# One Gram product for both lanes of a delta head, decays by ScalarE, and the next head's weight parts made inside the inversion

## The reference, cut to what matters

```
decay = exp(gc_i - gc_j) for i >= j           # gc: running sum of g in the chunk
lmat  = (beta_i * k_i . k_j) * decay, i > j   # strictly triangular
sol   = (I + lmat)^-1 [v * beta | k * beta * exp(gc)]        -> u, w
per chunk: v_new = u - w S;  o = (q exp(gc)) S + ((q k^T) * decay) v_new
           S = S * exp(gc_last) + (k * exp(gc_last - gc))^T v_new
```

## Time and profile before

| | |
|---|---|
| median of 3 runs | 4918.99 us (4915.6 to 4931.08) |
| the profiled execution's own time | 4920.18 us |
| its span | 4918.3 us |
| TensorE busy | 4060.4 us, 83% |
| VectorE busy | 3022.4 us, 61% |
| ScalarE busy | 1895.9 us, 39% |
| GpSimd busy | 768.2 us, 16% |
| mean granted TensorE clock | 0.894 of full speed |

### The profile page before, as it was taken

One profiled execution on the slowest core, in us unless ns is written; L12 is line 12 of the kernel. 1 busy time (PEld: TensorE's weight loads), 2 busy tenths in 40 slices (PEclk: granted clock), 3 DMA queues, 4 the chain that ended last, 5 costly groups with the idle time before them and its releaser, 6 DMA issues. The chain is left out here.

```text
span 4918.3 us, 52675 instructions
## 1 busy us (share of the span) xinstructions
PE 4060.4 (83%) x19068; PEld 3233.2 (66%) x19068; DVE 3022.4 (61%) x3602; ACT 1895.9 (39%) x2236; POOL 768.2 (16%) x364
## 2 busy tenths in 40 slices
PE   3956799958997999678888888849999597699995
PEld 2723587734734777467777877737888476588884
DVE  6753477344835874355555555538999543699995
ACT  2032332212203332333233323317777422477773
POOL 0200000001200000010000000013555100255551
PEclk9977899969998999778889888869999898799997
DMA  4310155211601452100000000019999510799993
GB/s 175 137 69 19 56 183 180 87 57 65 253 25 34 154 185 82 34 18 18 17 17 17 17 17 34 1 58 391 356 362 372 187 69 19 283 374 359 367 359 118
DMA packets 372150, 691.39 MB, mean 141 GB/s; under 512 B 38327, under 2 KB 118327, under 8 KB 371320
## 3 DMA queue, kind: packets, MB, share of 16 engines
q1 hardware_dynamic: 327696, 639.79, 36.5%
q10 hardware_dynamic: 25032, 32.98, 2.0%
q0 software_dynamic: 19296, 16.94, 1.0%
HBM read 700.01 MB, written 41.00 MB: 151 GB/s over the span
## 5 line engine op out<-in xcount | busy, mean ns | idle before, releaser
L505 PE MATMUL psum<-work_rounded 128*128 128x512 f32 x3504 | 1159.2, 401 | 119.6 <-DVE fixed_rounded L499 59.3
L499 DVE TENSOR_TENSOR ring_rounded<-ring,work_rounded 128x2048 fp32r<-128x2048 f32 (+1 forms) x445 | 816.0, 1836 | 422.9 <-ACT work_rounded L494 292.7
L505 PEld LDWEIGHTS psum<-work_rounded 128*128 128x128 f32 x3504 | 668.1, 192 | 282.5 <-issue 141.8
L505 PE MATMUL psum<-work_rounded,fixed_rounded 128*128 128x512 f32 x2544 | 781.6, 402 | 32.8 <-DVE fixed_rounded L2719 16.7
L505 PE MATMUL psum<-work_rounded,ring_rounded 128*128 128x512 f32 (+1 forms) x1824 | 726.4, 398 | 0.0
L2637 ACT ACTIVATE work_rounded<-ring 128x2048 fp32r<-128x2048 f32 x256 | 491.0, 1920 | 276.1 <-PE psum L505 173.1
L494 ACT ACTIVATE work_rounded<-ring 128x1024 fp32r<-128x1024 f32 x204 | 215.9, 1059 | 976.5 <-PE psum L505 711.6
L505 PEld LDWEIGHTS psum<-work_rounded,fixed_rounded 128*128 128x128 f32 x2544 | 482.6, 190 | 151.4 <-issue 22.2
L505 PE MATMUL psum<-fixed_rounded,work_rounded 128*128 128x512 f32 (+1 forms) x1088 | 431.1, 396 | 0.0
L505 PEld LDWEIGHTS psum<-work_rounded,ring_rounded 128*128 128x128 f32 x1824 | 351.1, 192 | 80.9
L499 DVE TENSOR_TENSOR work_rounded<-work,work_rounded 128x2048 fp32r<-128x2048 f32 (+1 forms) x196 | 337.8, 1733 | 41.5 <-ACT work_rounded L2637 37.6
(11 more groups left out here) (313 smaller groups left out, 6269.2 us busy)
## 6 DMA issues: line engine op xcount, KB each, us to landing
ring<-in_w SPq DMA_DIRECT2D x128, 2048.0 KB, 12.5
work<-in_w SPq DMA_DIRECT2D x64, 2048.0 KB, 12.0
ring<-in_mod_w SPq DMA_DIRECT2D x24, 2048.0 KB, 8.0
ring<-in_ada_w SPq DMA_DIRECT2D x24, 2048.0 KB, 7.9
ring<-in_ffn_w_in SPq DMA_DIRECT2D x44, 1024.0 KB, 7.6
ring<-in_ffn_w_out SPq DMA_DIRECT2D x10, 2048.0 KB, 7.8
ring<-in_w_in_a SPq DMA_DIRECT2D x32, 512.0 KB, 6.1
ring<-in_hy_w_in SPq DMA_DIRECT2D x6, 2048.0 KB, 8.0
```

Of the source, the lines that this page charges most:

```text
L499: return eng.tensor_tensor(c.rounded(v), v, c.rounded(v_high), ALU.subtract)
L505: ins = pe.matmul(out, c.rounded(w), c.rounded(x), start=(start and i == 0), stop=(stop and i == 2))
```

## The change

TensorE: the rows of lane 0 are made first, ahead of the transposes; those of lane 1 behind them. The product k k^T is made once for both lanes, without beta, and q k^T once; each head has thus 10 products where it had 20. Placing the start of the inverse in PSUM moves to each lane's first a. ScalarE: exp of the running sums per token (`eg`), and per lane six Relu instructions of 128x128 from PSUM with a bias and one Exp over 128x768 take the place of VectorE's arguments; the exponentials of the rows go to another buffer. The high parts of the next weights move from the opening to the ends of levels 1 to 4. VectorE: forms the matrix from decay, k k^T and the row of beta, without the triangle; it no longer makes the scaled copies; it makes the low parts of the weights at the ends of levels 2 to 5 (for head 0: ahead of the low parts of the inputs). GpSimd: copies z, makes the triangle for the scores, q times the exponentials, the mask of level 1, v times beta and a copy of k. In the scan the first product reads that copy of k and VectorE scales the product by -beta exp(gc) and adds v times beta. The semaphores `kb`, `darg`, `dexp`, `kdarg` go; `tt`, `eg`, `flat`, `m1`, `side` come. Of the removed lines only the first and last of long runs stand here; they are in the listing above.

```diff
-    def weights_high(self, act, h):
+    def weight_high(self, act, h, part):
         self.wait(act, h, "slab", 64)
-        for part in range(4):
...
-            low(self.c, pool, self.slab_dst()[:, part], self.slab_high[:, part]).then_inc(self.low, 1)
+        high(self.c, act, self.slab_high[:, part], self.slab_dst()[:, part]).then_inc(self.made, 1)
+    def weight_low(self, dve, h, part):
+        dve.wait_ge(self.made, 4 * h + (self.made0 + part + 1))
+        low(self.c, dve, self.slab_dst()[:, part], self.slab_high[:, part]).then_inc(self.low, 1)
     def gpsimd(self, pool):
-        self.weights_low(pool, 0)
         with pool.Fori(0, DHEADS - 1) as h:
-            self.weights_low(pool, h + 1)
+            self.pool_head(pool, h)
+            self.wait(pool, h, "end", 3)
+        self.pool_head(pool, DHEADS - 1)
+    def pool_head(self, pool, h):
+        s = self.s
+        def scores(l):
+            tri = self.c.const(("cum_f", "cum_b")[l]).unsqueeze(1).to_broadcast([P, NT, P])
+            self.wait(pool, h, "flat", l + 1)
+            pool.tensor_tensor(self.lane(l, L_QK, NT, P), self.lane(l, L_M, NTA, P)[:, NTC:NTA, :], tri, ALU.mult)
+        def grown(l):
+            last = P - 1 if l == 0 else 0
+            g = self.lane(l, L_KBG, KEYS)
+            self.wait(pool, h, "grown", l + 1)
+            pool.tensor_tensor(self.lane(l, L_QD, T), self.q, g[:, TC:KEYS], ALU.mult)
+            pool.tensor_copy(self.gl[:, l, :], g.rearrange("p (t n) -> p t n", n=P)[:, :, last])
+        def mask(l):
+            m = self.c.view(G_MASK + P * (7 * l + 1), P).unsqueeze(1).to_broadcast([P, NTA, P])
+            self.wait(pool, h, "tt", l + 1)
+            pool.sem_inc(self.settled, 1)
+            pool.drain()
+            pool.tensor_tensor(self.lane(l, L_M, NTA, P), self.lane(l, L_L, NTA, P), m, ALU.mult).then_inc(s["m1"], 1)
+        self.wait(pool, h, "silu", 5)
+        pool.sem_inc(self.settled, 1)
+        pool.tensor_copy(self.z_now, self.z)
+        scores(0)
+        grown(0)
+        mask(0)
+        scores(1)
+        mask(1)
+        grown(1)
+        self.wait(pool, h, "turned_out", 2)
+        pool.sem_inc(self.settled, 1)
+        pool.drain()
+        for l in range(2):
+            beta = self.beta[:, l, :].unsqueeze(2).to_broadcast([P, NTA, P])
+            pool.tensor_tensor(self.lane(l, L_KBG, NTA, P), self.vt, beta, ALU.mult)
+        pool.drain()
+        pool.tensor_copy(self.kz, self.k)
+        pool.drain().then_inc(s["side"], 1)
...
 def vector(self, dve):
+        for part in range(4):
+            self.weight_low(dve, 0, part)
...
+        def rows(l):
+            for t in range(NTA):
+                pe.matmul(c.pair(4 * l, KEYS)[:, P * t:P * t + P], self.g[:, l, t:t + 1].to_broadcast([P, P]),
+                          c.const(("cum_f", "cum_b")[l]), start=True, stop=True)
+                ins = pe.matmul(c.pair(4 * l + 2, KEYS)[:, P * t:P * t + P],
+                                self.beta[:, l, t:t + 1].to_broadcast([P, P]), ident, start=True, stop=True)
+            ins.then_inc(s["rows"], 1)
+        self.wait_mixed(pe, h, "cols", 1)
+        rows(0)
         self.wait(pe, h, "unit", 2)
         for t in range(NTA):
             ins = pe.transpose(c.pair(4, KEYS)[:, P * t:P * t + P], self.v[:, P * t:P * t + P], ident)
...
         for t in range(NTA):
             ins = pe.transpose(c.pair(6, KEYS)[:, P * t:P * t + P], self.k[:, P * t:P * t + P], ident)
         ins.then_inc(s["turned"], 1)
-        self.wait_mixed(pe, h, "cols", 1)
...
-            self.wait(pe, h, "kb", l + 1)
...
-            self.wait(pe, h, "mt", l + 1)
+        rows(1)
+        self.wait(pe, h, "grown", 1)
+        for t in range(NTA):
+            cols = slice(P * t, P * t + P)
+            ins = pe.matmul(c.pair(0, KEYS)[:, cols], self.k[:, cols], self.k[:, cols], start=True, stop=True)
+        ins.then_inc(s["kk"], 1)
+        self.wait(pe, h, "grown", 2)
+        for t in range(NTC, NTA):
+            ins = pe.matmul(c.ps[:, 4, P * (t - NTC):P * (t - NTC) + P], self.k[:, P * t:P * t + P],
+                            self.q[:, P * (t - NTC):P * (t - NTC) + P], start=True, stop=True)
+        ins.then_inc(s["kk"], 1)
+        def place(l):
+            self.wait(pe, h, "tt", l + 1)
             for t in range(NTA):
                 pe.matmul(c.pair(4 * l + 2, KEYS)[:, P * t:P * t + P], ident, self.lane(l, L_TT, NTA, P)[:, t, :],
                           start=(t % 4 == 0), stop=True, skip_group_check=True)
...
             for l in range(2):
                 i = 2 * v - 2 + l
                 T_, M = self.lane(l, L_T, NTA, P), self.lane(l, L_M, NTA, P)
-                self.wait(pe, h, "mt", i + 1)
+                if v == 1:
+                    place(l)
+                    self.wait(pe, h, "m1", l + 1)
+                else:
+                    self.wait(pe, h, "mt", i - 1)
                 self.wait(pe, h, "upd", i + 1)
...
+                    self.wait(pe, h, "side", 1)
                 else:
                     self.wait(pe, h, "s", i - 1)
-                pe.matmul(c.ps[:, 2 * l, 0:P], self.lane(l, L_KBG, NTA, P)[:, t, :], self.st(l, 0), start=True, stop=True)\
+                pe.matmul(c.ps[:, 2 * l, 0:P], self.kz[:, P * t:P * t + P], self.st(l, 0), start=True, stop=True)\
                     .then_inc(s["z"], 1)
...
     def scalar_head(self, act, h, more):
         c, s = self.c, self.s
+        self.wait_mixed(act, h, "cols", 1)
+        act.activation(self.eg, self.gcum, ACT.Exp).then_inc(s["eg"], 1)
+        def decay(l):
+            m, rows = self.lane(l, L_M, NTA, P), c.pair(4 * l, KEYS).rearrange("p (t n) -> p t n", n=P)
+            self.wait(act, h, "rows", l + 1)
+            for t in range(NTA):
+                act.activation(m[:, t, :], rows[:, t, :], ACT.Relu, scale=-1.0, bias=self.gcum[:, l, t:t + 1])
+            act.drain()
+            flat = self.lane(l, L_M, KEYS)
+            act.activation(flat, flat, ACT.Exp, scale=-1.0).then_inc(s["flat"], 1)
+        def grow(l):
+            act.activation(self.lane(l, L_KBG, KEYS), c.pair(4 * l, KEYS), ACT.Exp).then_inc(s["grown"], 1)
+        decay(0)
         self.wait(act, h, "turned", 2)
         act.activation(self.kt.rearrange("p t n -> p (t n)"), c.pair(6, KEYS), ACT.Copy).then_inc(s["turned_out"], 1)
-        for l in range(2):
...
-            self.weights_high(act, h + 1)
+        grow(0)
+        decay(1)
+        grow(1)
...
+            if more and v <= 4:
+                self.weight_high(act, h + 1, v - 1)
...
-        self.wait(dve, h, "silu", 5)
-        dve.tensor_copy(self.z_now, self.z)
         self.wait(dve, h, "turned", 1)
         dve.tensor_copy(self.vt.rearrange("p t n -> p (t n)"), c.pair(4, KEYS)).then_inc(s["turned_out"], 1)
+        self.wait(dve, h, "eg", 1)
+        dve.scalar_tensor_tensor(out=self.bg, in0=self.eg, scalar=-1.0, in1=self.beta, op0=ALU.mult, op1=ALU.mult)
+        ident = c.const("ident").unsqueeze(1).to_broadcast([P, NTA, P])
+        def mask(v, l, out):
+            m = c.view(G_MASK + P * (7 * l + v), P).unsqueeze(1).to_broadcast([P, NTA, P])
+            return dve.tensor_tensor(self.lane(l, out, NTA, P), self.lane(l, L_L, NTA, P), m, ALU.mult)
+        def decayed(l):
+            last = P - 1 if l == 0 else 0
+            self.wait(dve, h, "flat", l + 1)
+            dve.tensor_copy(self.kd[:, l, :], self.lane(l, L_M, NTA, P)[:, :, last])
+            self.wait(dve, h, "kk", 1)
+            dve.tensor_tensor(self.lane(l, L_L, KEYS), self.lane(l, L_M, KEYS), c.pair(0, KEYS), ALU.mult)
+            dve.drain()
+        def first(l):
+            v, TT = self.lane(l, L_L, KEYS), self.lane(l, L_TT, NTA, P)
+            dve.tensor_tensor(v, v, c.pair(4 * l + 2, KEYS), ALU.mult)
+            dve.drain()
+            mask(0, l, L_TT)
+            dve.drain()
+            dve.tensor_tensor(TT, TT, ident, ALU.add)
+            dve.drain().then_inc(s["tt"], 1)
+        decayed(0)
+        first(0)
+        dve.transpose(self.lane(0, L_T, KEYS), self.lane(0, L_TT, KEYS))
+        decayed(1)
+        dve.drain().then_inc(s["upd"], 1)
+        first(1)
+        self.wait(dve, h, "kk", 2)
         for l in range(2):
-            kb, m = self.lane(l, L_T, KEYS), self.lane(l, L_M, NTA, P)
...
-            dve.drain().then_inc(s["upd"], 1)
+            qk = self.lane(l, L_QK, T)
+            self.wait(dve, h, "m1", l + 1)
+            dve.tensor_tensor(qk, qk, c.ps[:, 4, :], ALU.mult)
+        dve.transpose(self.lane(1, L_T, KEYS), self.lane(1, L_TT, KEYS))
+        dve.drain().then_inc(s["upd"], 1)
         for v in range(1, LEVELS):
             if v < LEVELS - 1:
                 for l in range(2):
                     self.wait(dve, h, "a", 2 * v - 1 + l)
-                    mask(v + 1, l).then_inc(s["mt"], 1)
+                    mask(v + 1, l, L_M).then_inc(s["mt"], 1)
...
+            if more and 2 <= v <= 5:
+                self.weight_low(dve, h + 1, v - 2)
...
```

(60 more changed lines are left out.)

39 lines of the change are left out of this document (5 added, 34 removed).

## The result

The change takes 4859.78 us (median of 4 runs, 4855.3 to 4862.75) against 4920.4 for the kernel before (4 runs): ratio 0.9873, 95% interval 0.9855 to 0.9891. The forecast was 4874 with a range of 4851 to 4900.

The account below looks back on a forecast made before the run. Openings were taken as a chain across engines ending on VectorE, stretched by GpSimd; the inversion as limited by ScalarE's copies. -84.3 + 16 + 27.2 - 4.0 = -45.1 us from 4920.2 gives 4875.1, as median 4874; range 4851 to 4900.

Parts of the forecast that it names:

- The opening: Head start, VectorE's first small copy to lane 1's transpose: 38.95 to 27.5 us (last head 31.4 to 27.2), -84.3 in all.
- no stretch: Opening: VectorE operations beside GpSimd's mask and scores, mostly reading PSUM, were taken as not slowed by GpSimd.
- The 7.6 us: Old opening: four VectorE operations stretched beside GpSimd's low parts; the third head's opening exceeds the last's by 7.6 us.
- The levels: Inversion, levels 1 to 4: one unhidden ScalarE high part of 0.97 us each, 3.9 us a head, 27.2 in all.
- The loss behind the opening: Level 1: masks held by GpSimd or low TensorE clock, not adding; 2.0 us a head (0 to 5), 16 in all.
- Ahead of head 0: Before the first head: VectorE's input low parts end sooner without GpSimd beside them, gaining 4.0 us (1 to 5).
- Rival 1: Behind the opening: clock stays high or held masks are hidden, so no losses there; 4850 us, chance 0.18.
- Rival 2: Losses are large: GpSimd slower than scaled, low clock reaches the placements; three us a head more, 4898, chance 0.23.
- Rival 3: GpSimd becomes the bound of the opening; slower than before, 4934 us at 4 us an instruction, chance 0.06.
- Rival 4: ScalarE: Relu and Exp change the table each time, four more loads a head; 4895 us, chance 0.06.

Follow-up runs that it names:

- e1: Kernel before, with only the low parts of the next weights moved from GpSimd to VectorE at the ends of levels 2 to 5: 4850.0 us, ratio 0.9857.
- e3: Changed kernel with ScalarE's four high parts put back at the end of the opening: 4838.2 us, ratio 0.9834.
- e6: Changed kernel with 19 idle products, which nobody reads, in TensorE's gaps behind the Gram product: 4868.3 us, ratio 0.9886.
- e8: e7 plus the idle products of e6 in TensorE's gaps: 4823.5 us, ratio 0.9799.
- e7: Changed kernel with high parts back in the opening and GpSimd's v, beta products and copy of k behind level 2's masks: 4833.6 us, ratio 0.9819.

## Why the prediction was right

**The opening** was forecast at 27.5 us and is 26.9; the sum over the heads was forecast at -84.3 and is -84.7. The chain is the one that was forecast, but that the sum agrees so closely is luck, for errors cancel in two places.

- The forecast took the third head's 38.95 us for all seven looped heads, whose mean before is 38.4. That is 3.6 us too much in the sum; openings 0.55 us shorter than the 27.5 gave 3.9 back.
- Inside the opening, VectorE starts on the Gram product 12.9 us after its first copy (2403.48 less 2390.54) and not 14.65. The 24 instructions of lane 0's rows took 4.4 us and not 5.15, since the clock rose from 0.50 to 1.00 among them; the six Relu took 1.66 and not 1.9. Then 1.0 us is lost again, where the forecast added no stretch: the small copy ahead of lane 1, which takes 0.17 us alone, takes 1.10 beside GpSimd's mask of lane 0. And GpSimd's instruction over 768 columns takes 1.81 us and not 1.5 (2.4 ns a column where the fp32r rows gave 2.1).

The 7.6 us read from the earlier trace rows for GpSimd's presence are the 7.9 us of e1. What the forecast did not say is how little is left for the rest of the new opening: 3.6 us a head.

**The levels** were forecast at +3.9 us a head and are 3.8 (e3). This was the best supported term, since TensorE was waiting on ScalarE with no gap in the earlier trace rows.

**The loss behind the opening** was taken as 2.0 us a head, held masks and low clock not adding. It is 0.7 us in the three heads where the clock stayed high and 1.6 in the other five, about 10 us for the 16 forecast; the reason holds, the size was off. With 26.4 us for the high parts (27.2 forecast) this is the +36.7.

**Ahead of head 0**, from ScalarE's first high part to its first evacuation, it is 14.5 us against 17.9, so -3.4 (forecast 4.0), and the low parts account for it: e1 has 14.75. Another 2.7 us went between there and head 0, and 1.9 had gone before the stage was reached, where nothing was changed.

**What the forecast lacked** is the clock at the end of a head, which it counted at nothing: "The scan keeps its number and kinds of instructions." Here are the same 20 products, of one column each, in the kernel before, where the granted clock is 0.51 over them, and then in the changed one, where it is 1.00:

```profile
2396.77 4.32 PE L1798 MATMUL psum<-fixed,work 128*128 128x1 f32 x20 [2.13 <-ACT work L1839]
```

```profile
2378.19 2.39 PE L1848 MATMUL psum<-fixed,work 128*128 128x1 f32 x20 [2.13 <-ACT work L1889]
```

Tails are 16.1 to 20.0 us after and 17.5 to 20.0 before, with the same work in them, and their length goes with the clock: in these two kernels 20.0 us at a mean of 0.60, 18.8 at 0.69, 17.5 at 0.81 and 16.2 at 0.89. The last head's scan is 18.9 us at 1.00, or 21.7 to 21.9 at 0.73, in every kernel here. And the 2.7 us ahead of head 0 came with a clock of 0.95 where it was 0.86. In the profiled execution the forecast's sum was short by 19.8 us. The tails (7.1), the last scan (2.8) and this stretch (2.7) are 12.6 of it; 6.5 are the inversions, and 1.9 came ahead of the stage, less small terms the other way. In the tails and in this stretch the instructions are unchanged, and e1, with the old scan, has the short last scan too. Whether the change brings this phase of the clock about, no run separates, and it could not be worked out from the trace before; e6 has longer tails (18.9) and the longer last scan.

**The rivals.** Rival 1, no losses behind the opening, came true in part: the clock stayed high there in three looped heads, but even these lose 0.7 us. Rival 2 was right that GpSimd is slower than was scaled, 1.81 us for 1.5, but nothing like three us a head came of it. Rival 3, GpSimd as the bound, did not happen: VectorE waits for it 1.24 us once an opening. Rival 4, that Relu and Exp change the table, did not either: there are three loads a head as before, 1.28 us each. The Trainium skill says that relu is in every table set ("ScalarE: Activation LUTs", "Table sets: the hidden batching unit"), and this trace agrees.

## What to carry to other kernels

Before crediting a rewrite, run its smallest part alone: here one moved helper gave 69 us, and the rest of the change took about 10 back. Moved work is hidden only under a wait that is still there after the change: ScalarE's wait in the opening could hold all four high parts (e3), while between two copies of a chain each one costs nearly its full length (0.94 us of level for 0.97 of work). And when two causes delay the same instruction, remove each alone and both together before judging either. Last, a total that agrees with the forecast can hide errors that cancel: compare the parts.

## What was not expected of the hardware

A stretch of the same work differs by up to 4 us (tails) with the granted clock, from head to head within one execution, so single heads must not be compared, and even means over seven heads differ by 1 to 2 us with it. A VectorE copy of 128x6 took 1.10 us beside a GpSimd operation of 1.81 us, and 0.17 alone. Idle products in TensorE's gaps went with a clock of 1.00 behind the opening in every head of e6 and e8, gave every head the short inversion, and shortened level 1 by 1.6 us where nothing else held it (e7 to e8); yet the same products in e6 came with longer tails.
